# Two moving halves in one matmul for the late first-layer pieces of layer 0, with copies on ScalarE and adds on GpSimd; modulation sums as columns; another order in the second block's mixer

## The reference, cut to what matters

```python
# first block, each layer l
mod = cond @ ada_w[l] + ada_b[l]                 # 6 * 1024 numbers: sh1, sc1, g1, sh2, sc2, g2
x = x + g1 * (y @ w_out[l])
h = rms_norm(x, norm2_g[l]) * (1.0 + sc2) + sh2
# peer_ffn: 16384 experts, computed densely here
pre = h @ u.T;  act = gelu(pre) * gate;  x = x + g2 * (act @ v)
# second block, hybrid_mixer
parts = split(h @ w_in)                          # q, k, v of the window, selected and compressed branches, gates, retention
s_w = softmax(q @ kw.T ...); s_s = softmax(q @ ks.T ...); gates = sigmoid(...)
```

## Time and profile before

| | |
|---|---|
| three runs | 3313.51, 3314.51 (median), 3315.90 us |
| the profiled execution | 3316.16 us, of which 3314.3 us from its first to its last instruction (the span) |
| PE busy | 3248.8 us, 98% of the span |
| DVE, ACT, POOL busy | 2440.5, 1581.9, 106.2 us |
| mean granted TensorE clock | 0.994 |
| HBM read | 650.66 MB, 207 GB/s over the span |

### The profile page before, as it was taken

How to read it: one execution, slowest core, us unless ns; L and a number is a source line. 1 busy time by engine, 2 the same in 40 slices (tenths; PEclk the granted TensorE clock), 3 DMA queues, 4 the chain that set the end, 5 groups by cost and what they waited for, 6 DMA issues and landing times.

```text
span 3314.3 us, 51087 instructions
## 1 busy us (share of the span) xinstructions
PE 3248.8 (98%) x20524; PEld 2875.9 (87%) x20524; DVE 2440.5 (74%) x3563; ACT 1581.9 (48%) x1899; POOL 106.2 (3%) x32
## 2 busy tenths in 40 slices
PE   7999999999999999999999999999999999999999
PEld 4889999888889899998888888888888888888887
DVE  7879996777887769986667777666667576666675
ACT  4544554343335544554443345455554454555553
POOL 0015000000000032000000000000000000000000
PEclk9999999999999999999999999999999999999999
DMA  9455577778884344675667775544445555444453
GB/s 379 173 200 180 205 247 276 273 275 286 283 281 171 108 172 179 229 275 204 216 217 241 239 263 196 196 149 151 165 162 187 189 196 202 154 153 162 158 191 140
DMA packets 172164, 689.66 MB, mean 208 GB/s; under 512 B 12396, under 2 KB 78724, under 8 KB 99223
## 3 DMA queue, kind: packets, MB, share of 16 engines
q1 hardware_dynamic: 167492, 663.86, 55.8%
q10 hardware_dynamic: 4436, 22.53, 1.9%
HBM read 650.66 MB, written 35.68 MB: 207 GB/s over the span
## 4 chain that ended last, share of the span: by engine, by line
PE 64%; DVE 2%; ACT 1%; DVEq 1%; issue 1%; ACTq 0%
PE ps L944 12%; PE ps L1293 10%; PE ps L995 8%; PE ps L892 7%; PE ps L950 6%; PE ps L1002 4%; PE ps L898 3%; PE ps L914 3%; PE ps L920 1%; PE ps L1254 1%; DVE weights_lower L2080 1%; PE ps L1027 1%; PE ps L939 1%; ACT weights_upper L1560 1%; PE ps L964 1%
## 5 line engine op out<-in xcount | busy, mean ns | idle before, releaser
L1560 ACT ACTIVATE weights_upper<-weights 128x2048 fp32r<-128x2048 f32 x520 | 997.0, 1918 | 1481.7 <-issue 515.0
L2080 DVE TENSOR_TENSOR weights_lower<-weights,weights_upper 128x2048 fp32r<-128x2048 f32 x498 | 1139.2, 2289 | 487.5 <-ACT weights_upper L1560 486.8
L892 PE MATMUL ps<-hT_span,weights_upper 128*128 128x256 f32 x4352 | 548.3, 284 | 0.0
L892 PEld LDWEIGHTS ps<-hT_span,weights_upper 128*128 128x128 f32 x4352 | 531.7, 192 | 4.8 <-issue 3.5
L944 PE MATMUL ps<-hT_span,weights_upper 128*128 128x512 f32 x1664 | 397.3, 391 | 0.0
L944 PEld LDWEIGHTS ps<-hT_span,weights_upper 128*128 128x128 f32 x1664 | 305.8, 188 | 59.2
L898 PE MATMUL ps<-hT_span,weights_lower 128*128 128x256 f32 x2240 | 291.6, 283 | 1.6 <-DVE weights_lower L2080 1.6
L898 PEld LDWEIGHTS ps<-hT_span,weights_lower 128*128 128x128 f32 x2240 | 278.9, 192 | 1.8 <-DVE weights_lower L2080 1.8
L1293 PE MATMUL ps<-weights_upper,hidden_lower 128*128 128x512 f32 x1008 | 250.7, 391 | 0.0
L1293 PE MATMUL ps<-weights_upper,hidden_upper 128*128 128x512 f32 x1008 | 248.9, 389 | 0.0
L1293 PE MATMUL ps<-weights_lower,hidden_upper 128*128 128x512 f32 x1008 | 248.9, 389 | 0.0
(11 more groups left out here) (429 smaller groups left out, 4127.6 us busy)
## 6 DMA issues: line engine op xcount, KB each, us to landing
weights<-in_parts SPq DMA_DIRECT2D x264, 1024.0 KB, 4.8
weights<-in_experts SPq DMA_DIRECT2D x256, 1024.0 KB, 4.9
scr<-gates SPq DMA_DIRECT2D x32, 1024.0 KB, 8.2
work<-in_ada_s SPq DMA_DIRECT2D x96, 256.0 KB, 5.3
gates<-h SPq DMA_DIRECT2D x16, 1024.0 KB, 4.8
gates<-work SPq DMA_DIRECT2D x16, 1024.0 KB, 4.8
weights<-in_ada_w SPq DMA_DIRECT2D x6, 2048.0 KB, 15.3
scr<-in_ada_l SPq DMA_DIRECT2D x35, 256.0 KB, 6.7
```

The lines of the kernel that those rows point to most:

```text
L892: m = mm(bank[:, e * T:(e + 1) * T], up[:, c, e * P:(e + 1) * P], src[1 - n][:, c, :], start=(e == 0 and n == 0 and c == 0), stop=False, s ...
L1560: f(upper[:, p_.r % SPLIT, :], raw[:, p_.r, :], ACT.Copy).then_inc(upper_ready, 1)
L2080: v.tensor_tensor(lower[:, s, :], raw[:, p_.r, :], upper[:, s, :].bitcast(F32), ALU.subtract)\
```

## The change

1. Layer 0's 24 first-layer pieces of the turns use `doubled`. Each takes a second bank: `Ux0` is bank 1 for u = 0, `Ux1` is bank 3 for u = 1. ACT copies all four quarters (two to their place, two to `second_sums`), GpSimd adds them in SBUF, and ACT applies Gelu to the sum in the next step.
2. Each modulation row becomes four columns: four matmuls with the accumulator as the stationary operand, every fourth column of it, and a column of ones moving. ACT copies 128 x 4, and one DMA writes 16 bytes for each partition.
3. `late_sum` and `late_take` of tiles 2 and 3 are gone. In layer 0 `shifted_transposes` multiplies the unsummed accumulators by ones, so that the matmul itself sums.
4. In the second block `nsv` stands ahead of `wS`, two of the four `ret` parts ahead of `lS`, ACT takes the last two `ret` parts ahead of the second group of exponentials, and a one-element sigmoid is put ahead of the gates' sigmoid.

```diff
-    late(2, 3)
-        if before and layer == 0 and u == 1 and t >= AHEAD:
+        if layer == 0 and u == 1 and t >= AHEAD:
             p.fill("Ux1", 1, bank=3 - t, parts=1, start=t)
...
+            p.fill("nsv", 2, parts=2)
             p.fill("wS", NSA_H)
-            p.fill("nsv", 2, parts=2)
+            p.fill("ret", 2, parts=1)
             p.fill("lS", NSA_H)
-            p.fill("ret", 4, parts=1)
+            p.fill("ret", 2, parts=1, start=2)
...
+                k = at(firsts[l], 0)
+                for t in range(AHEAD, TURNS if l == 0 else AHEAD):
+                    for u in range(2):
+                        second = ("Ux1", t) if u else ("Ux0", 0, t - AHEAD)
+                        g.wait_ge(*k.emptied("U", u, t))
+                        g.wait_ge(*k.emptied(*second))
+                        g.sem_inc(S("held"), 1)
+                        for e in range(2):
+                            mine = gact[t % AHEAD][:, u, e, :]
+                            m = g.tensor_tensor(mine, mine, second_sums[e], ALU.add)
+                        m.then_inc(S("hidden_sum"), 1)
...
-                    if t < AHEAD or l == 0:
+                    if t < AHEAD:
                         by_feature(expert_part(l, 0, n), k.bank("U", u), hT1)
...
-                            mm(k.bank("row", tile)[0:1, :], ones[:, 0:1], ada_acc[tile % 2], start=True, stop=True,
-                               skip_group_check=True).then_inc(k.fill_sem("row", tile), 1)
+                            acc = ada_acc[tile % 2].rearrange("k (p b) -> k b p", b=4)
+                            for b in range(4):
+                                m = mm(k.bank("row", tile)[:, b:b + 1], acc[:, b, :], ones[:, 0:1], start=True,
+                                       stop=True, skip_group_check=True)
+                            m.then_inc(k.fill_sem("row", tile), 1)
...
-                    if i == 3:
-                        late_sum(2, 3)
-                for j in range(2, 4 if l == 0 else 2):
-                    pe.wait_ge(*k.emptied("late", j))
-                shifted_transposes(k, "h2T", h, mod[:, 3 * D:4 * D], "norm_diag", 2 * l * TT)
+                if l == 0:
+                    pe.wait_ge(S("late_used"), 4 * KC)
+                shifted_transposes(k, "h2T", h, mod[:, 3 * D:4 * D], "norm_diag", 2 * l * TT,
+                                   rows=None if l else ones[:, 0:1])
...
-                late_take(2, 3)
...
+                    if l == 0:
+                        if 2 * (t - AHEAD) + u:
+                            act.wait_ge(S("hidden_sum"), 2 * (t - AHEAD) + u)
+                        for e, emptied in enumerate((k.empty_sem("U", u), k.empty_sem(*second))):
+                            f(mine[:, e, :], banks[e][:, 0:T], ACT.Copy)
+                            f(second_sums[e], banks[e][:, T:2 * T], ACT.Copy).then_inc(emptied, 1)
+                        return
...
+                parts_by_token(k, l, "nsv", 0, 0, cols=280)
                 pe.wait_ge(*k.emptied("nin", 5))
                 all_scores("wS", 2)
-                parts_by_token(k, l, "nsv", 0, 0, cols=280)
+                for i in range(2):
+                    parts_by_feature(k, l, "ret", i)
                 all_scores("lS", 0)
-                for i in range(4):
+                for i in range(2, 4):
                     parts_by_feature(k, l, "ret", i)
...
+                f(stat(322, 1), EPS1_COL, ACT.Sigmoid)
...
-                softmax_exp(sel, NSA_H, 88, 104, "lmax", l + 1, "lexp")
                 for i in range(2):
                     ahead("ret", 2 + i)
                     take(k, "ret", 2 + i, kr[:, 2 * i:2 * i + 2, :])
+                softmax_exp(sel, NSA_H, 88, 104, "lmax", l + 1, "lexp")
```

More of the change, by code:

```diff
@@ L177, in plan_first @@
     p.fill("U", 1, bank=1, times=TURNS, parts=1, start=1)
-    if before:
-        p.fill("Ux0", 1, bank=1, times=TURNS - AHEAD, parts=1)
+    p.fill("Ux0", 1, bank=1, times=TURNS - AHEAD, parts=1)
     for n, (layer, t, u) in enumerate(expert_order()):
-        if before and layer == 0 and u == 1 and t >= AHEAD:
+        if layer == 0 and u == 1 and t >= AHEAD:
             p.fill("Ux1", 1, bank=3 - t, parts=1, start=t)
@@ L554, in two_mixers_and_peer_then_nsa_retention_memory @@
         ada_bias_row = view(scr, 0, NBLK)
-        ada_row = [scr[0:1, c:c + NBLK // 2] for c in (512, 5888)]
+        ada_column = [st[:, 328 + 4 * j:332 + 4 * j] for j in range(2)]
+        second_sums = [view(scr, 512, T), view(scr, 5888, T)]
         def ada_sub(s):
@@ L732, in keep_row @@
                     sp.wait_ge(*k.emptied("row", tile))
-                    for b in range(2):
-                        c = tile * NBLK + b * (NBLK // 2)
-                        sp.dma_start(ada_dram[0:1, c:c + NBLK // 2], ada_row[b]).then_inc(ada_kept[b], 16)
+                    sp.dma_start(ada_dram[0:1, tile * NBLK:(tile + 1) * NBLK].rearrange("o (p b) -> (o p) b", b=4),
+                                 ada_column[tile % 2]).then_inc(ada_kept[tile % 2], 16)
                 for n, (layer, t, u) in enumerate(expert_order()):
@@ L843, in scaled_transposes, with shifted_transposes @@
                             m.then_inc(k.fill_sem(name, i), 1)
-            def shifted_transposes(k, name, src, shift, signal, value):
+            def shifted_transposes(k, name, src, shift, signal, value, rows=None):
                 for i in range(4):
@@ L852, in shifted_transposes @@
                         mm(k.bank(name, i)[:, e * T:(e + 1) * T], shift[:, c * P:(c + 1) * P],
-                           ident[:, 0:1].broadcast_to([P, T]), start=(e == 0), stop=False, skip_group_check=True)
+                           (ident[:, 0:1] if rows is None else rows).broadcast_to([P, T]), start=(e == 0),
+                           stop=False, skip_group_check=True)
                 for t in range(TT):
@@ L1739, in gelu @@
                     mine = gact[t % AHEAD][:, u, :, :]
-                    if t < AHEAD or l == 0:
+                    if t < AHEAD:
                         f(mine, k.bank("U", u), ACT.Gelu).then_inc(k.empty_sem("U", u), 1)
                         return
-                    banks = k.bank("U", u), k.bank(*(("Ux1", t) if u else ("Ux0", 0)))
+                    second = ("Ux1", t) if u else ("Ux0", 0)
+                    banks = k.bank("U", u), k.bank(*second)
+                    if l == 0:
[5 more added lines that the diff above has]
+                        return
                     for e in range(2):
@@ L1768, in ada_take @@
                     act.sem_inc(S("held"), 1)
-                    for b in range(2):
-                        if tile:
-                            act.wait_ge(ada_kept[b], 16 * tile)
-                        m = f(ada_row[b], k.bank("row", tile)[0:1, b * (NBLK // 2):(b + 1) * (NBLK // 2)], ACT.Copy)
-                    m.then_inc(k.empty_sem("row", tile), 1)
+                    if tile >= 2:
+                        act.wait_ge(ada_kept[tile % 2], 16 * (tile // 2))
+                    f(ada_column[tile % 2], k.bank("row", tile)[:, 0:4], ACT.Copy)\
+                        .then_inc(k.empty_sem("row", tile), 1)
                 for n, (layer, t, u) in enumerate(expert_order()):
@@ L1793, in _ @@
                             row1_in(1)
-                    if l and n > 2 * AHEAD and expert_order()[n - 1][0] == 0:
+                    if n > 2 * AHEAD and expert_order()[n - 1][0] == 0:
                         gelu_of_sum(*expert_order()[n - 1][1:])
@@ L2828, in combine @@
                     v.drain()
+                ahead("nsv", 0)
                 maxima("wS", near, 24, "wmax")
-                ahead("nsv", 0, 2)
+                ahead("nsv", 1)
+                ahead("ret", 0)
                 maxima("lS", sel, 72, "lmax")
-                ahead("ret", 0, 4)
+                ahead("ret", 1, 3)
                 for i in range(RH):
```

8 lines of the change are left out of this document (4 added, 4 removed).

## The result

The changed kernel takes 3321.24 us (median of 14 runs, 3317.47 to 3324.43) against 3313.53 of the kernel before (14 runs, 3312.61 to 3316.30): ratio 1.002, 95% interval 1.0013 to 1.0027, so 4 to 9 us **slower**. Executions of one kernel differ by several us (the two slowest of the changed kernel, at 3324, had a mean granted clock of 0.992, the fastest, at 3317, one of 0.995), so one profile of each kernel need not show the whole difference of two medians.

A forecast was written before the change was run, and what follows sets the result against it. PE, busy 98% of the span, was taken as the bound. Terms -5.0 + 4.1 - 0.5 - 1.2 - 7.7 = -10.3 us moved the median from 3314.5 to 3304.2 us, range 3299 to 3312.

The forecast's parts named there:

- doubled pairs: Layer 0's turns on PE: 12 pairs of first-layer pieces fall from 11.52 to 11.10 us each, -5.0 us.
- waits ahead of tiles 2 and 5: Layer 0's turns: PE waits 2.05 us, twice, for ACT's Gelu and four copies to free bank 3, +4.1 us.
- lowered clock behind them: PE at 1.2 GHz after the two bank 3 waits: taken as 0, since PE is dense on both sides.
- shift of layer 0: Two late sums leave PE ahead of layer 0's shift; the diagonal on DVE then limits: -1.2 us, between -1.0 and -1.7.
- second block: Both layers' stretch to `rS` takes 37.3 us in the new order: -3.1 and -4.6, together -7.7 us.
- sums as columns: Twelve modulation sums on PE: eight records at 0.114 us make 0.91 against a row's 0.95, -0.5 us.
- The rival beside it: Strided columns load slowly: at twice the record's price the sums cost 10.9 us more, 3315.1; chance 0.08.
- the rival of 0.12: The two row waits in layer 0's turns also lower the clock, 1.6 us each: 3307.4; chance 0.12.
- one new wait in `wS`: Second block: heads 7 and 8 of `wS` wait 1.1 us for `nsv`'s banks, which ACT frees late.
- the 0.8 taken: Layer 0's turns: one GpSimd add of 256 columns takes 0.8 us, between 0.6 and 4.6, and nothing shows.
- the cast: DVE cast of 512 columns, 0.43 us alone, 3.64 beside GpSimd's subtraction; so DVE may be held up to one add.
- the 9.5 from which ACT would have held PE: Rival that GpSimd can't keep up: two adds over 9.5 us make ACT's queue hold PE, 3340; chance 0.05.

## Why the prediction was wrong, point by point

| term | forecast | in the profiles |
|---|---|---|
| doubled pairs, 12 x (11.51 - 11.11) | -5.0 | -4.9 (4.3 in time) |
| waits ahead of tiles 2 and 5 | +4.1 | +4.3 (2 x 1.91, and 2 x 0.23 for the start behind them) |
| lowered clock behind them | 0, priced as a rival | +3.1 (12.56 + 12.61 - 2 x 11.03) |
| bank 3 behind the sums of tiles 1, 4, 7 | not seen | +1.6 (3 x (0.63 - 0.10)) |
| columns | -0.5 | +8.5 (12 x 0.71) |
| shift of layer 0 | -1.2 | -1.1 |
| second block | -7.7 | -6.9 (41.94 + 40.37 - 2 x 37.70) |
| sum | -10.3 | +4.6; the spans differ by +4.2, the medians by +7.7 |

What the terms leave over is small: PE comes to the first changed place 0.7 later than in the kernel before, and in the turns ten runs of second-layer pieces are 0.07 to 0.10 shorter each, 0.9 in all.

**The step that failed first** is "sums as columns". It priced a record at 0.114 from a row whose weights lie side by side, and said itself that no row had a strided stationary operand. The rival beside it had the right size, twice the record's price (0.228; measured 0.234 from load to load), but got a chance of 0.08, although it cited the rule that fits the runs (the Trainium skill, Advanced Engine Details and Errata, Memory Cachelines, says that an access pattern with a different line for each access pays a penalty). "Nothing in the trace speaks for or against it" is no reason for so little: the term's value had been taken from the only end that favoured the change. Halfway between the record's price and twice that, 12 x 8 x 0.057 = 5.5 us more, the sum would have been -4.8 us, 3309.7, and no "faster". This step accounts for 9.0 of the 14.9 us between the forecast's terms and the profiles'.

**The second** is the clock. The forecast had the row that a wait of this length was followed by a stretch at 1.2 GHz, and set it aside because PE is dense on both sides of the new waits. It is dense there, and the clock fell all the same, behind both: 3.1 us, as the rival of 0.12 had it. The rivals were priced one at a time, too: strided columns and lowered clock together are 3304.2 + 10.9 + 3.2 = 3318.3 by the prediction's own prices, most of the way to the 3321.2.

**The third** was seen from one side only. The text asked for each sum whether bank 3 is empty when the sum comes, and found two that wait. It didn't ask the same for the pieces, which now wait for the sums to be taken out. ACT takes a sum behind a whole `upper`: the timeline of ACT behind tile 1's sum, which PE ends at 589.69, is

```profile
593.69 1.91 ACT L1575 ACTIVATE weights_upper<-weights 128x2048 fp32r<-128x2048 f32 x1 [5.32 <-PE ps L925]
595.51 0.15 ACT L1793 ACTIVATE stats<-ps 128x4 f32<-128x4 f32 x1
```

and the second piece of that pair, due at 595.4 (1.91 behind 593.44, as in a pair without a sum), starts at 595.76, 0.1 behind the end of the take. The profile names no engine for this wait (`issue`); that it is the bank follows from the kernels without the shared bank, whose pairs behind a sum have only the 0.1 of any sum.

**What held.** The doubled pairs, the two waits with their place and cause (1.91 against 2.05), the shift (the diagonal is late next, as said: PE waits 0.4 for it), and the walk through the second block with its one new wait in `wS` (0.71 idle in both layers, 1.1 forecast). GpSimd kept up, and ACT's list of waits has none for it, though its adds are longer than the 0.8 taken. DVE's modulation pieces fall into two groups: the 48 that run beside an add take 1.04 to 1.06 us, the other 48 take 0.75 as in the kernel before. So such a piece is held for 0.3 us, where the prediction allowed up to a whole add, by the cast:

```profile
L805 POOL TENSOR_TENSOR rowp<-rowp,scr x12: 1131/1190/1599, 596.9 to 654.0; 128x256 f32<-128x256 f32 x12
```

```profile
L2570 DVE SCALAR_TENSOR_TENSOR scr<-work,stats,scr x96: 750/898/1058, 528.4 to 948.1; 128x512 f32<-128x512 f32 x96
```

Two adds take at most 2.7 us together, far under the 9.5 from which ACT would have held PE.

## What to carry to other kernels

Where a change gives an instruction a layout that no row shows, its price is open, and the forecast's value must not be the end that the change hopes for; here weights 4 and 8 bytes apart loaded alike, and 16 bytes apart took 1.7 times as long. When a buffer gets a second user, ask on both sides who waits: the new user for the old one's consumer, and the old one for the new one's. A change that is sound in its parts can still lose by where it puts two small sums: with every second column as weights and five sums moved, the same change is 8 to 17 us faster than the kernel before.

## What the runs showed of the hardware that was not expected

- fp32 weights of 128 columns load in 192 ns side by side, 196 ns 8 bytes apart, and 329 ns 16 bytes apart.
- A column sum with contiguous weights (0.81 us) is cheaper than the row sum of the same numbers (0.95 us).
- 2 KB to DRAM landed in 5.3, 7.9 and 11.9 us in pieces of 16, 8 and 4 bytes, and the loads on the same queue got late: with the sums in place DVE waited 29.8 us for them with pieces of 4 bytes, 0.5 with pieces of 8, and not at all with 16.
- PE's waits of 1.9 us between dense work were followed by a stretch at a granted clock of 0.50 (1.2 GHz) in 7 of 8 cases, at a cost of 1.4 to 1.6 us each.
- A DVE operation of 512 columns with two inputs in SBUF took 1.05 us beside a GpSimd add of 256 columns and 0.75 elsewhere; the adds took 1.19 at the median and 0.81 at the least.
